# Moving tiles at three distances from the weights in a float32 two-block transformer

## What is computed

```python
# first block, twice
z = rmsnorm(x) @ w_in                       # 1024 -> 1280: Fourier part, q, k, v, memory queries
y = concat(rms(fourier(zf)), rms(window_attn(q, k, v)), rms(memory_attn(zm, rmsnorm(mem) @ w_mem_kv)))
x = x + rmsnorm(y @ w_out)
gate, up = split(rmsnorm(x) @ w_ffn_in)     # 1024 -> 2 x 2816
x = x + rmsnorm((silu(gate) * up) @ w_ffn_out)

# second block, twice
x = x + 0.5 * swiglu(rms_norm(x, ffn1_norm), ffn1_w1, ffn1_w2)        # 2816 wide
proj = rms_norm(x, mix_norm) @ w_in + b_in                            # 1024 -> 6 parts
merged = gates[0] * y_a + gates[1] * y_b + gates[2] * y_c             # recurrence, latent attention, convolution
x = x + merged @ w_out
x = x + 0.5 * swiglu(rms_norm(x, ffn2_norm), ffn2_w1, ffn2_w2)
# after both layers: rms_norm(x, final_norm)
```

## Time and profile before

| | |
|---|---|
| median of three executions | 3464.14 us (3461.09 to 3464.89) |
| span of the profiled execution | 3464.2 us |
| TensorE busy, matmuls | 3364.4 us, 97%, 19557 instructions |
| TensorE busy, weight loads | 2886.5 us, 83% |
| VectorE / ScalarE / GpSimd busy | 71% / 47% / 2% |
| mean granted TensorE clock | 0.994 |
| DMA | 325 MB, 94 GB/s |

### The profile page before, as it was taken

The page is one execution under the profiler, slowest core; times in us unless marked ns, Lnnn a source line. Parts: engine busy times, 40 slices in busy tenths (PEclk is TensorE's granted clock), DMA queues, the critical chain, the costliest instruction groups (busy, mean ns, idle before and its releaser), DMA issues. The chain is left out here.

```text
span 3464.2 us, 49516 instructions
## 1 busy us (share of the span) xinstructions
PE 3364.4 (97%) x19557; PEld 2886.5 (83%) x19557; DVE 2451.1 (71%) x3500; ACT 1628.3 (47%) x2399; POOL 67.0 (2%) x96
## 2 busy tenths in 40 slices
PE   7999999999999999999999999999999989999999
PEld 5679988768998899887678899889988757788997
DVE  8669854759872988467885698458864888658863
ACT  4645643445652556335523365336542562335642
POOL 1000000000000000000000000000000000000000
PEclk9999999999999999999999999999999999999999
DMA  4123323213332333232132333333333212223332
GB/s 141 50 73 110 110 87 110 92 44 92 110 110 97 92 106 115 94 101 65 54 97 86 98 106 102 101 106 108 101 104 108 71 49 85 85 97 98 110 104 85
DMA packets 341371, 325.25 MB, mean 94 GB/s; under 512 B 31960, under 2 KB 312356, under 8 KB 341156
## 3 DMA queue, kind: packets, MB, share of 16 engines
q1 hardware_dynamic: 335588, 307.95, 28.0%
q0 software_dynamic: 3776, 12.45, 1.6%
q10 hardware_dynamic: 1792, 1.88, 0.2%
HBM read 313.84 MB, written 2.10 MB: 91 GB/s over the span
## 5 line engine op out<-in xcount | busy, mean ns | idle before, releaser
L2168 DVE TENSOR_TENSOR w_lo<-raw,w_hi 128x2048 fp32r<-128x2048 f32 x190 | 435.2, 2291 | 482.7 <-ACT w_hi L1524 482.4
L1524 ACT ACTIVATE w_hi<-raw 128x2048 fp32r<-128x2048 f32 x190 | 363.8, 1915 | 835.5 <-PE products L799 582.7
L799 PE MATMUL products<-a_hi,w_hi 128*128 128x512 f32 (+1 forms) x1216 | 489.6, 403 | 12.1 <-DVE a_lo L2228 9.5
L799 PE MATMUL products<-a_hi,w_lo 128*128 128x512 f32 (+1 forms) x1216 | 476.3, 392 | 0.0
L799 PE MATMUL products<-a_lo,w_hi 128*128 128x512 f32 (+1 forms) x1216 | 475.5, 391 | 0.0
L940 PE MATMUL products<-seven_x,w_hi 128*128 128x256 f32 x2592 | 464.5, 280 | 2.4 <-DVE w_lo L2467 2.3
L940 PEld LDWEIGHTS products<-seven_x,w_hi 128*128 128x128 f32 x2592 | 395.0, 188 | 4.1 <-DVE w_lo L2467 3.6
L940 PE MATMUL products<-seven_x,more_hi 128*128 128x256 f32 x1632 | 376.1, 280 | 5.6 <-ACT rs_b L1636 5.6
L940 PE MATMUL products<-seven_x,w_lo 128*128 128x256 f32 x1296 | 361.5, 279 | 0.0
L799 PEld LDWEIGHTS products<-a_hi,w_hi 128*128 128x128 f32 (+1 forms) x1216 | 229.3, 189 | 69.0 <-issue 16.5
L940 PEld LDWEIGHTS products<-seven_x,more_hi 128*128 128x128 f32 x1632 | 277.5, 188 | 6.8 <-ACT rs_b L1636 6.8
(11 more groups left out here) (465 smaller groups left out, 7242.8 us busy)
## 6 DMA issues: line engine op xcount, KB each, us to landing
raw<-in_ffn_w SPq DMA_DIRECT2D x244, 512.0 KB, 4.2
raw<-in_w_in SPq DMA_DIRECT2D x108, 512.0 KB, 4.6
raw<-in_w_ffn_in SPq DMA_DIRECT2D x88, 512.0 KB, 4.3
raw<-in_w_ffn_out SPq DMA_DIRECT2D x40, 512.0 KB, 4.5
raw<-in_w_out SPq DMA_DIRECT2D x32, 512.0 KB, 4.0
raw<-in_ffn_w SPq DMA_DIRECT2D x24, 384.0 KB, 3.6
x_sums<-x_sums POOLq DMA_DIRECT2D x12, 512.0 KB, 5.9
raw<-in_w_mem_kv SPq DMA_DIRECT2D x8, 512.0 KB, 3.9
```

The lines of the kernel that those rows point to most:

```text
L799: mm = pe.matmul(G[pair][0:m, into + b, 0:n], w[:, s, at:at + m], x, start=(first or into > 0) and k == 0 and q == 0, stop=(last or ends) ...
L1524: act.activation(w_hi[:, s, :], raw[:, s, :], ACT.Copy).then_inc(hi_ready, 1)
L2168: dve.tensor_tensor(w_lo[:, s, :], raw[:, s, :], w_hi[:, s, :].bitcast(F32), ALU.subtract).then_inc(lo_ready, 1)
```

## The change

Three constants give each family of tiles a distance of its own, in bytes, from a multiple of 512. `ODD_A` = 64 is for the operand `a_hi`/`a_lo`. `ODD_H` = 480 is for the gated layer `h_hi`/`h_lo`, for its full-precision tile `h_full`, and for the memory's `m_hi`/`m_lo`. `ODD_Y` = 96 is for everything in region B of the second block's mixer: the branches `ya`, `yb`, `yc`, the merged rows `mg`, and the tiles that share that region, such as `xa`, `gate_w`, `glu`, `conv` and the heads. The counters are set so that the next region begins where it must not overlap; the `early` tiles move up by 512 bytes and `h_lo`'s region grows by 1 KB. The weights, `seven_x`, `late_hi`, `more_hi` and `more_lo` stay. No instruction is added, removed or moved in order.

```diff
+ODD_A, ODD_H, ODD_Y = 64, 480, 96
...
-    a_hi = place("a_hi", [P, DC, SEQ], F32R)
-    a_lo = place("a_lo", [P, DC, SEQ], F32R)
+    a_hi = place("a_hi", [P, DC, SEQ], F32R, at=REGION_A + ODD_A)
+    a_lo = place("a_lo", [P, DC, SEQ], F32R, at=REGION_A + 16 * KB + ODD_A)
+    top[0] = REGION_A + 32 * KB
...
     REGION_B = top[0]
-    h_hi = place("h_hi", [P, FC, SEQ], F32R)
-    top[0] += LINE
+    h_hi = place("h_hi", [P, FC, SEQ], F32R, at=REGION_B + ODD_H)
+    top[0] = REGION_B + 44 * KB + LINE
     H_LO = top[0]
-    h_lo = place("h_lo", [P, FC, SEQ], F32R)
+    h_lo = place("h_lo", [P, FC, SEQ], F32R, at=H_LO + ODD_H)
+    top[0] = H_LO + 45 * KB
...
-    early_hi = place("early_hi", [P, 3, QUAD], F32R, at=H_LO + 32 * KB)
-    early_lo = place("early_lo", [P, 3, QUAD], F32R, at=H_LO + 38 * KB)
+    early_hi = place("early_hi", [P, 3, QUAD], F32R, at=H_LO + 32 * KB + LINE)
+    early_lo = place("early_lo", [P, 3, QUAD], F32R, at=H_LO + 38 * KB + LINE)
...
-    h_full = place("h_full", [P, FC, SEQ], at=H_LO)
+    h_full = place("h_full", [P, FC, SEQ], at=H_LO + ODD_H)
...
+    b1[0] += ODD_H
     m_hi = in_b("m_hi", [P, DC, MEM], F32R)
     m_lo = in_b("m_lo", [P, DC, MEM], F32R)
...
-    b1[0] = REGION_B
+    BRANCHES = REGION_B + ODD_Y
+    b1[0] = BRANCHES
     yc_hi = in_b("yc_hi", [P, LC, SEQ], F32R)
...
-    glu = place("glu", [P, LC, SEQ], at=REGION_B)
-    conv = place("conv", [P, LC, SEQ], at=REGION_B + 8 * KB)
+    glu = place("glu", [P, LC, SEQ], at=BRANCHES)
+    conv = place("conv", [P, LC, SEQ], at=BRANCHES + 8 * KB)
```

More of the change, by code:

```diff
@@ L320, in two_blocks @@
     more_lo = place("more_lo", [P, 5, QUAD], F32R, at=REGION_A + 10 * KB)
-    early_hi = place("early_hi", [P, 3, QUAD], F32R, at=H_LO + 32 * KB)
-    early_lo = place("early_lo", [P, 3, QUAD], F32R, at=H_LO + 38 * KB)
+    early_hi = place("early_hi", [P, 3, QUAD], F32R, at=H_LO + 32 * KB + LINE)
+    early_lo = place("early_lo", [P, 3, QUAD], F32R, at=H_LO + 38 * KB + LINE)
     more_sums = place("more_sums", [P, 5, QUAD], at=REGION_A + 10 * KB)
-    early_sums = place("early_sums", [P, 3, QUAD], at=H_LO + 38 * KB)
+    early_sums = place("early_sums", [P, 3, QUAD], at=H_LO + 38 * KB + LINE)
     x_sums = place("x_sums", [P, 11, 4 * HALF], at=REGION_B + ODD)
-    h_full = place("h_full", [P, FC, SEQ], at=H_LO)
+    h_full = place("h_full", [P, FC, SEQ], at=H_LO + ODD_H)
     X_SUMS = {"B11": 1, "T3": 3, "T2": 5, "B12": 6, "T4": 7, "B21": 8, "T1": 9, "B22": 10}
@@ L422, in two_blocks @@
     lru_in = in_b("lru_in", [P, LC, SEQ])
-    glu = place("glu", [P, LC, SEQ], at=REGION_B)
-    conv = place("conv", [P, LC, SEQ], at=REGION_B + 8 * KB)
+    glu = place("glu", [P, LC, SEQ], at=BRANCHES)
+    conv = place("conv", [P, LC, SEQ], at=BRANCHES + 8 * KB)
     craw_sq = place("craw_sq", [P, 5, SEQ], at=REGION_T)
[L426 to L429, removed]
+    lru_tmp = place("lru_tmp", [P, 3, SEQ], at=BRANCHES + 26 * KB)
+    craw = place("craw", [P, 6, SEQ], at=BRANCHES + 32 * KB)
+    gate_w = place("gate_w", [P, LC, 2, P], at=BRANCHES + 44 * KB)
+    mla_prob.append(place("mla_prob4", [P, ROWS_4], at=BRANCHES + 34 * KB))
     mla_prob.append(place("mla_prob5", [P, ROWS_4], at=REGION_T))
```

## The result

The changed kernel takes 3496.07 us (median; 3494.65 to 3499.36) beside 3464.51 us for the kernel before (3461.09 to 3469.84): a ratio of 1.0093, 95% interval 1.0079 to 1.0107. It is slower by 31.6 us. The forecast was 3437.0 us, and the upper end of the range, 3490, is too low as well.

The account below looks back on a forecast made before the run. TensorE was taken to bound the kernel through the spacing of its matmuls; 8748 matmuls x 3.1 ns = 27.1 us off 3464.1 us gave 3437.0 us, with an overall range of 3398 to 3490 us.

Parts of the forecast that it names:

- What bounds the kernel: Whole kernel: TensorE, busy 3364.4 of 3464.2 us at 2.4 GHz; time is matmul count times the distance between starts.
- The counts: Dense stages: 8556 matmuls with 512 columns and 192 with 256 get another distance; L940 keeps its own.
- 3.1 ns gained for each matmul: All 8748 shifted matmuls: the 256-column gain, 120.0 ns at distance 0 to 116.9 at 32, applied to each; 27.1 us.
- the cleanest test: L838 with `h` as weights, at L940's distance of +32: 100 us should hold about 449 matmuls instead of 443.
- 32 is nearer to these distances than 128 is: Shifted matmuls: reason for using L940's gain at 32 rather than the rotary unit's loss at multiples of 128.
- The bad end: Shifted matmuls: at worst 4.6 ns lost each, from the rotary-key unit's row of 24 matmuls with 96 output rows, 231.3 ns.
- The good end: Shifted 512-column matmuls: at best 216.0 ns, without the extra reads, a gain of 10.7 ns each.
- The slower one: L799 and L838: 8508 matmuls lose 4.6 ns, 39.1 us, giving 3502.6 us; counts of 435 or less; chance 26%.
- The rival's condition: Shifted matmuls: the kernel gets slower once more than 40% of them fall on the losing side; `a` at 64 is 46%.
- More with more distance: Shifted matmuls: each 32 bytes worth 3.1 ns, so 64 gives 6.2 and 96 gives 9.3; 46.8 us, 3417 us; chance 17%.
- Nothing happens: Shifted matmuls: no distance matters, or gains and losses cancel; time stays 3464 us; chance 17%.
- What doesn't move: Other engines and DMA: same sizes and bytes, no wait added; the 99.8 us of TensorE not busy left whole.

Follow-up runs that it names:

- experiment 6: Computation left out, matmul streams alone at distances 0, 32, 64 and 192 with 17 column counts from 192 to 512; at distance 0, 111.6 ns (192) to 226.7 (512).
- experiment 5: Streams alone, moving tile 0 to 252 bytes away in steps of 4, then 32 to 128 weight columns at eight distances; 512 columns with 128 weight columns: 226.7 to 240.0 ns.
- experiment 1: Computation left out, streams of 96 matmuls alone at multiples of 32 bytes; 512 columns 226.7 ns at distance 0, 233.3 at 32; 256 columns 120.0 and 116.7.

## Why the prediction was wrong

- *What bounds the kernel.* Right: the number of matmuls times the distance between their starts, nothing else. The loss is in TensorE's busy time alone, its idle time fell by 3.2 us, and the clock was full in the stretches compared. Not complete: short stretches at 1.2 GHz, 11.9 us between the start and the last matmul, are hidden in the slices that I read as full.
- *The counts.* Right: 8556 matmuls with 512 columns and 192 with 256 got another distance, L940 none, and exactly these changed.
- *The step that failed* is the 3.1 ns gained for each matmul, "as if it were paid once per weight load and not per column". I had one measured distance, 32, with 256 columns, and one equality, an extra of 13.3 ns at distance 0 with either number of columns, and took from the second that the first could be carried over. The equality is true and is a coincidence of these two sizes (at distance 0 the extra is 11.7 ns with 288 columns and 16.7 with 496, experiment 6): at 32 the extra is 10.0 with 256 columns and 20.0 with 512. `h` as weights, which I had called the cleanest test, has just that distance and went from 226.7 to 233.3 ns. "32 is nearer to these distances than 128 is" failed as well: no distance says anything of its neighbour (226.7 at 28, 233.3 at 32).
- *The bounds.* The bad end, 4.6 ns lost, was not an end: a constant distance lost 6.6. Nor was the row what I took it for. Its matmuls have 96 weight columns, and streams with 96 of them take 230.0 ns at distance 0 and 231.7 at 128 (experiment 5). So the row mixes three things, the distance, the number of weight columns and the jumps of the distance, and is no measure of the first. The better row lay right ahead of it: the 24 matmuls of the same unit with 128 weight columns, whose distance jumps in the same way, start at 1593.05, which is (1598.63 - 1593.05) / 24 = 232.5 ns, 5.8 more than at distance 0. The good end, 10.7 ns, is reached nowhere with 512 columns.
- *The rivals.* The slower one happened, with its place (L799 and L838), its sign (516 matmuls of `h` in 120 us are 430 in 100, below its 435) and its reason: distance 0 is a good state with 512 columns. Its 4.6 ns were too little for `h`, `mg`, `y` and `a` as weights (6.2 to 6.6) and too much for `a` moving (2.2), and the two errors nearly cancel: its sum was 39.1 us, and 39.3 by families is what the trace shows. The time came out at 3496 and not 3502.6 by terms that the sum didn't have: TensorE stands 3.2 us less, which the prediction had left whole, and the changed kernel's executions lose some 3 us less at the lower clock. In the earlier trace rows each slice of the clock shows a 9, and I took that for full. The rival's condition, that over 40% of the matmuls lose, was met by 100% of those with 512 columns. I gave it 26% since the distance of that unit "jumps every three matmuls"; what I should have weighed is that no row with 512 columns showed a gain, and the short ones are 192 of 8748.
- *More with more distance* fell: `a` at 64 lost least and `mg` at 96 as much as `h` at 32. *Nothing happens* fell: two tiles in a memory that nothing else used gave 226.7 or 233.4 ns by their distance alone (experiment 1). The Trainium skill (SBUF — State Buffer, Who interferes with whom) says that TensorE's read ports are independent and that it waits on no one; for TensorE's own two reads these streams are against it.
- The other rule cited, the Trainium skill's gap of columns / 2.4 plus 2.5 ns (TensorE: Matmul & The Clock Gate, Back-to-back issue gap), is not reached by any of the streams: 226.7 at the least with 512 columns, against 215.8. The page gives it for an isolated matmul, which the prediction doesn't say; for a stream of weight loads and matmuls it states about 131 ns at 512 columns, and these float32r streams are further from that.
- *The range* ended at 3490 by leaving out "where nearly everything loses 4.6 ns", 13%. With 6.6 ns as an unknown beyond the bound it should have reached over 3500.
- *What doesn't move* held: VectorE and ScalarE kept their busy times, DMA moved the same 325.25 MB, and no wait took over.

## What to carry to other kernels

A spacing measured at one number of columns and one distance holds for that pair and not for another, and the number of weight columns belongs to it as well. Before tiles are shifted, a stream of a hundred matmuls with the real tile offsets, columns and weight columns tells the spacing; only the offset of moving against stationary tiles modulo 256 has to be varied. Each stream is worth running more than once and then checking in the kernel, as one distance can have two spacings. In this kernel 512-column matmuls with 128 weight columns are best left at distance 0, where 226.7 ns was the least of all 64 distances, while 256-column ones gain 6.7 ns of 120.0 at 192, as long as they take the better of its two spacings. And when a sum rests on a gain measured at another number of columns, and no row of the right shape shows it, the gain is not a term yet.

## What the runs showed that was not expected

- The spacing of split matmuls depends on the distance of the two tiles modulo 256 bytes, in a pattern without order: 226.7 to 240.0 ns with 512 columns, 113.3 to 130.0 with 256 (experiments 1 and 5). Moving both tiles together changes nothing, and it is there without any traffic of other engines. With fewer weight columns the pattern is another, and at 32 of them as wide.
- A distance can have two spacings, and a stage keeps the one it has: 228.9 or 233.3 ns for `a` at 64, 116.7 or 117.8 for L940 at 32, 113.3 or 117.8 at 448. What picks it is open; streams of one kernel with nothing beside them show both too (256 columns at 192).
- From 224 columns down to 192, the fewest tried, the columns no longer count: 111.7 ns for both.
- TensorE's clock fell to 1.2 GHz for a few microseconds in the middle of a kernel that keeps it busy for 97% of the time, 11.9 us lost in the profiled execution of before. Some lie where it stands part of the time (it is busy for 7.50 of 10 us in the window 1640 to 1650 of after), others in a window in which it is busy throughout (1610 to 1620 of before, after 9.06 of 10 us in the window ahead of it).
